# Expert retrieval of an encoder layer: a one-hot part on ScalarE, other shares of gathered rows for DVE and TensorE, V loaded four tiles at a time

## The reference

```python
D_MODEL, SEQ, PEER_HEADS, PEER_KEYS, PEER_TOPK = 1024, 1024, 8, 128, 16

def reference(x, c, ...):
    ...                                   # adaLN modulation, HGRN2 and convolution groups, w_out
    hn2 = _modulate(_rmsnorm(h, norm_ffn_g[l]), sh2, sc2)
    ffn = _peer(hn2, peer_wq[l], peer_keys1[l], peer_keys2[l], peer_u[l], peer_v[l])
    h = h + g2[:, None, :] * ffn
    ...                                   # final RMSNorm, shift and scale

def _peer(h, wq, keys1, keys2, u_tab, v_tab):
    q = (h @ wq).reshape(nb, L, PEER_HEADS, PEER_DKEY)
    s1, s2 = ...                          # scores of both halves of q against 128 keys each
    v1, i1 = lax.top_k(s1, PEER_TOPK); v2, i2 = lax.top_k(s2, PEER_TOPK)
    cand = v1[..., :, None] + v2[..., None, :]
    sc, ci = lax.top_k(cand, PEER_TOPK)   # 16 of 16384 experts for each head
    e = i1[ci // 16] * PEER_KEYS + i2[ci % 16]
    w = jax.nn.softmax(sc, axis=-1)
    # for each token, over its 128 experts:
    act = gelu(sum_d h[t, d] * u_tab[e[t, j], d])
    y[t] = sum_j (w[t, j] * act) * v_tab[e[t, j]]
```

## Time and profile before

| | us |
|---|---|
| median of 3 runs (lowest to highest) | 3291.83 (3290.16 to 3292.69) |
| the profiled execution | 3279.82 |
| its span, first to last instruction | 3278.1 |
| PE busy, DVE busy, ScalarE busy | 2959.7, 2363.2, 553.7 |
| mean granted clock of TensorE | 0.945 |

### The profile page before, as it was taken

One profiled execution on the slowest core, in us unless ns is written; L12 is line 12 of the kernel. 1 busy time (PEld: TensorE's weight loads), 2 busy tenths in 40 slices (PEclk: granted clock), 3 DMA queues, 4 the chain that ended last, 5 costly groups with the idle time before them and its releaser, 6 DMA issues. The chain is left out here.

```text
span 3278.1 us, 31019 instructions
## 1 busy us (share of the span) xinstructions
PE 2959.7 (90%) x10396; PEld 1592.4 (49%) x10396; DVE 2363.2 (72%) x4478; ACT 553.7 (17%) x682; POOL 1220.6 (37%) x1104
## 2 busy tenths in 40 slices
PE   6999699759689997899999999996899998999995
PEld 2557577547475443444554454443344443444442
DVE  4796445530587889999999998886677666776674
ACT  3011443321221100222221221221000000000003
POOL 0111111021124545344333335554455454555550
PEclk8998899869798998999999999998899999999997
DMA  4441111013237999899899899999999999999993
GB/s 184 175 161 35 58 32 34 26 53 108 84 96 296 412 414 337 308 322 348 304 333 333 311 324 379 414 415 408 392 402 399 402 400 402 401 400 402 399 378 141
DMA packets 299657, 919.78 MB, mean 281 GB/s; under 512 B 27376, under 2 KB 76784, under 8 KB 296176
## 3 DMA queue, kind: packets, MB, share of 16 engines
q0 software_dynamic: 147456, 536.94, 42.6%
q1 hardware_dynamic: 113408, 301.76, 25.1%
q10 hardware_dynamic: 38640, 79.18, 6.3%
HBM read 830.21 MB, written 87.56 MB: 280 GB/s over the span
## 5 line engine op out<-in xcount | busy, mean ns | idle before, releaser
L1451 PE MATMUL s_pu<-s_hn,s_ut 128*128 128x512 f32 x2304 | 1017.1, 597 | 7.5 <-ACT s_gst L1562 5.2
L1406 POOL DMA_INDIRECT s_slot<-in_u,s_row x512 | 516.6, 1009 | 714.7 <-DVE s_slot L1807 628.8
L1406 POOL DMA_INDIRECT s_slot<-in_v,s_row x512 | 551.3, 1077 | 452.8 <-DVE s_hB L1820 348.1
L1451 PEld LDWEIGHTS s_pu<-s_hn,s_ut 128*128 128x128 f32 x2304 | 437.4, 192 | 543.7 <-issue 539.8
L1807 DVE SCALAR_TENSOR_TENSOR s_slot<-s_slot,s_ph 128x1024 f32<-128x1024 f32 x512 | 612.5, 1220 | 104.1 <-DMA s_slot<-in_u,s_row 85.0
L1820 DVE SCALAR_TENSOR_TENSOR s_hB<-s_slot,s_dot,s_hB 128x1024 f32<-128x1024 f32 x445 | 561.8, 1284 | 128.0 <-DMA s_slot<-in_v,s_row 127.4
L296 PE MATMUL s_ps<-hn_hi,w_hi 128*128 128x512 f32 x704 | 290.9, 413 | 93.5 <-PEq L270 57.1
L1536 PE MATMUL s_pw<-s_ct,s_vt 128*128 128x512 f32 x512 | 249.1, 610 | 49.5 <-DVE s_ct L1828 25.1
L297 PE MATMUL s_ps<-hn_lo,w_hi 128*128 128x512 f32 x704 | 282.0, 401 | 0.0
L1536 PE MATMUL s_ph<-s_ct,s_vt 128*128 128x512 f32 x512 | 242.5, 596 | 16.0 <-DVE s_slot L1807 16.0
L1536 PE MATMUL s_pu<-s_ct,s_vt 128*128 128x512 f32 x512 | 242.2, 595 | 0.0
(11 more groups left out here) (280 smaller groups left out, 2994.7 us busy)
## 6 DMA issues: line engine op xcount, KB each, us to landing
s_ut<-in_u_tiles SPq DMA_DIRECT2D x128, 512.0 KB, 7.2
s_vt<-in_v SPq DMA_DIRECT2D x128, 512.0 KB, 24.0
s_g<-s_gst ACTq DMA_DIRECT2D x128, 256.0 KB, 7.0
s_w<-s_wb ACTq DMA_DIRECT2D x16, 2048.0 KB, 10.9
s_gr<-s_g SPq DMA_DIRECT2D x64, 512.0 KB, 23.7
s_wr<-s_w SPq DMA_DIRECT2D x16, 2048.0 KB, 46.6
s_ada<-in_ada SPq DMA_DIRECT2D x48, 512.0 KB, 5.4
s_x<-in_xT SPq DMA_DIRECT2D x16, 512.0 KB, 4.0
```

The costliest lines, as they stand in the source:

```text
L1406: pool.indirect_dma_start(out=slot[s][:, :], out_offset=None, in_=io[kind], in_offset=bass.IndirectOffsetOnAxis(ap=row[b][:, j:j + 1], axi ...
L1451: mm = pe.matmul(pu[:, n % 2, :], ut[n % UR][:, k, :], hn[:, k, :], start=(k == 0), stop=(k == DC - 1))
```

## The change

ScalarE makes the third weighted part, `hotw[..][2]`, in 8 activations of 128 columns with the remainder of the weight (`rest`, fp32) as scale; DVE makes two parts in place of three, and `hot1` has two buffers. PE waits for this part with a semaphore of its own (`third_ready`), and the cast of the third part falls away. PE gets 48 side rows, DVE 976 rows in all in place of 960. `sparse_by` gives 164 rows by tile 20, 387 by tile 97, 507 by tile 122 and 537 by tile 127. V comes in 32 loads of four tiles (2 MB, 16 KB runs, from a copy of V laid out for that), into two slots.

```diff
-SIDE_ROWS = 64
+SIDE_ROWS = 48
...
     for t in range(-QT, n + 1):
-        tenths += (45 if t < RANK_AT else 42 if t < HOT_AT[0] else
-                   26 if t < RANK_AT + RANK_TILES * (len(RANKED) - MADE_PICKS) else 47 if t < 123 else 60)
+        tenths += (45 if t < RANK_AT else 44 if t < HOT_AT[0] else
+                   29 if t < RANK_AT + RANK_TILES * (len(RANKED) - MADE_PICKS) else 48 if t < 123 else 60)
...
-    VR = 8
+    VG, VR = 4, 2
...
-    hot1 = at("s6_hot1", [P, 4, KEYS, 2], BF16, F0 + 48 * KB)
+    hot1 = [at(f"s6_hot1{s}", [P, 4, KEYS, 2], BF16, F0 + (48, 60)[s] * KB) for s in range(2)]
...
-    vt = [at(f"s6_vt{s}", [P, D], F32, F0 + 4 * KB * s) for s in range(VR)]
+    vt = [at(f"s6_vt{s}", [P, VG, D], F32, F0 + 4 * VG * KB * s) for s in range(VR)]
...
             def load_v(n):
+
                 if n >= VR:
-                    sp.wait_ge(v_done, n - VR + 1)
-                sp.dma_start(vt[n % VR][:, :], io["v"][n * P:(n + 1) * P, :]).then_inc(v_in[n % VR], 16)
+                    sp.wait_ge(v_done, VG * (n - VR + 1))
+                sp.dma_start(vt[n % VR][:, :, :], io["v_tiles"][n]).then_inc(v_in[n % VR], 16)
...
-            for n in range(KEYS - VR):
-                load_v(n + VR)
+            for n in range(KEYS - VG * VR):
+                if n % VG == VG - 1:
+                    load_v(n // VG + VR)
...
             def place_batch(a, r):
                 n = 16 * a + r
                 pe.wait_ge(hot_ready, n + 1)
+                pe.wait_ge(third_ready, n + 1)
...
-                pe.wait_ge(v_in[n % VR], 16 * (n // VR + 1))
+                pe.wait_ge(v_in[n // VG % VR], 16 * (n // (VG * VR) + 1))
...
+            def third_parts(a, r):
+                n = 16 * a + r
+                act.wait_ge(hot1_ready, n + 1)
+                if n >= 2:
+                    unit = UNITS * ((n - 2) // 16) + 2 + 2 * ((n - 2) % 16)
+                    act.wait_ge(pw_full[unit % 2], unit // 2 + 1)
+                for i in range(8):
+                    q, t = divmod(i, 2)
+                    o = act.activation(hotw[n % 2][2][:, q, :, t], hot1[n % 2][:, q, :, t], ACT.Copy,
+                                       scale=rest[:, 1, 8 * r + i:8 * r + i + 1])
+                o.then_inc(third_ready, 1)
...
+                for a, r in hot_batches(n - 1):
+                    third_parts(a, r)
                 for a, r in hot_batches(n - 2):
                     evacuate(a, r)
...
-                dve.tensor_copy(wT[2][:, :], rest[:, 1, :])
-                dve.drain()
...
-                dve.tensor_tensor(hot1[:, :, :, :], keys, spread(keyT[0]), ALU.is_equal)
+                dve.tensor_tensor(hot1[n % 2][:, :, :, :], keys, spread(keyT[0]), ALU.is_equal).then_inc(hot1_ready, 1)
                 dve.tensor_tensor(hot2[n % 2][:, :, :, :], keys, spread(keyT[1]), ALU.is_equal)
                 dve.drain()
-                for x in range(3):
-                    dve.tensor_tensor(hotw[n % 2][x][:, :, :, :], hot1[:, :, :, :], spread(wT[x]), ALU.mult)
+                for x in range(2):
+                    dve.tensor_tensor(hotw[n % 2][x][:, :, :, :], hot1[n % 2][:, :, :, :], spread(wT[x]), ALU.mult)
...
+        "v_tiles": a["peer_v"][0].reshape(KEYS // 4, 4, KEYS, D).transpose(0, 2, 1, 3),
```

More of the change, by code:

```diff
@@ L1299, in step6 @@
     keyT = [small(f"keyT{s}", [P, P], BF16) for s in range(2)]
-    wT = [small(f"wT{x}", [P, P], BF16) for x in range(3)]
+    wT = [small(f"wT{x}", [P, P], BF16) for x in range(2)]
     rest = small("rest", [P, 2, P])
@@ L1321, in step6 @@
         sd_made, sd_taken, sd_stored = sem("s6_sd_made"), sem("s6_sd_taken"), [sem(f"s6_sd_stored{s}") for s in range(2)]
-        hot_ready = sem("s6_hot_ready")
+        hot_ready, hot1_ready, third_ready = sem("s6_hot_ready"), sem("s6_hot1_ready"), sem("s6_third_ready")
         pw_full = [sem(f"s6_pw_full{s}") for s in range(2)]
@@ L1535, in _ @@
                             pe.wait_ge(taken, number["u", SPARSE - 1, P - 1] + 1)
-                    mm = pe.matmul(bank(c), vt[n % VR][:, c * P:(c + 1) * P], ct[:, n % CR, :],
+                    mm = pe.matmul(bank(c), vt[n // VG % VR][:, n % VG, c * P:(c + 1) * P], ct[:, n % CR, :],
                                    start=(n == 0), stop=(n == KEYS - 1))
```

## The result

The changed kernel takes 3261.08 us (median of 3 runs, 3254.38 to 3263.82); the kernel before took 3291.83 (3290.16 to 3292.69). The ratio is 0.990, with a 95% interval of 0.9884 to 0.9916: 31 us faster. The time lies inside the range (3233 to 3271), but 15 us above the forecast of 3246 and 3 above the likeliest case's own range (3234 to 3258). The profiled execution took 3261.08 with a span of 3259.4, only 18.7 less than the profiled execution of before (3279.8). That difference misleads, as the second trace of before shows further down.

What follows compares the result with a forecast made beforehand. It took PE and DVE as full from 1307 to 1985 us, then DMA, then PE with waits for V. 0 - 16.0 - 22.4 - 7.6 = -46.0 us from 3291.8 gave 3246; range 3233 to 3271 with 8 of 10.

Steps and rivals of the forecast that it cites:

- the likeliest case: The forecast itself for the whole kernel: 3246 us, own range 3234 to 3258, chance 0.66.
- start of products: End of first phase: DVE's products start at 2286 as now, change 0, bounds 2280 and 2295 (-6 to +9).
- Part by part, first phase: DVE, ScalarE and PE up to the last u tile: it ends 8 to 14 us sooner, worth nothing by itself.
- the 12 us of room: At tile 93 PE could place its batch 12 us earlier before it waits for DVE.
- These cancel: DVE by tile 97: 30 us saved on weighted parts against 31 us spent on 26 more u rows.
- The stall (-16.0): PE's 15.97 us idle after the first V tile goes, as no u row stands between products: -16.0 us.
- the waits for V (-22.4, -7.6): V phase: 22.4 of 24.4 us of PE's waits and 7.6 of 8.9 us of slow running go.
- V is on time, and PE becomes the bound: V phase: with V at 320 GB/s, eight tiles' loads take 54.5 us, under PE's 54.9.
- (a): V loads: large rows get only half the bytes, no larger share; about -24 us, 3268; chance 0.14.
- (b): Phase change: ScalarE or the `take_y` wait delays DVE by 9 us, few V waits stay; -32 us, 3260; chance 0.08.
- (c): From 1985 to 3220 us full DMA engines are the bound whatever PE waits for; no gain, 3290; chance 0.05.
- (d): V phase: V's halved headway makes it slower, +65 us or 3357; chance 0.07 together with dear third parts.

Runs made afterwards that it cites:

- the second trace of before: The kernel before, unaltered, run and profiled once more: 3290.0 us, ratio 1.0 (0.9987 to 1.0012); profiled execution 3298.2 us, span 3296.5.

## Why the prediction came out as it did

The direction and the mechanism in the V phase were right. The term that was mis-sized is the start of products, put at 0: against the trace that the sum was made from the u tiles come no earlier, and the chain behind them is 17 us longer. Counted from u tile 0 the start is 14 to 18 us later; -46 with that gives -32 to -28, an estimate from one trace of before, and -31 was measured.

*Part by part, first phase.* "PE then ends the u tiles 8 to 14 us sooner, about 2250" is the step that came out short. PE gained 10 us from tile 24 to tile 97 (652 us to 642 and 643), near the 12 us of room that I gave it. The four rows ahead of the first batch cost the 5 us that I had named: tiles 0 to 24 take 205 us, for 200 in the three other traces with the old quota, though the first trace of before has 206. Behind tile 97, where I had nothing, the change has 279 and 282 us for 270 in the first trace of before; PE waits there 3.5 and 10.9 us for ScalarE, where the first trace of before shows no such wait. From tile 0 to tile 127 that is 1127 and 1131 us, for 1129 in the first trace: no gain. The second trace of before, with 31 us for its stop taken off, has 1136, so 5 to 9 us sooner by that one. "These cancel" holds for DVE's time (30 us saved, 31 spent on rows), but with the new quota DVE is the pace-maker from tile 24 to 97: without ScalarE's part the end is 26 us later. I had priced the whole first phase at 0. A row made there is 0.52 MB that need not be moved later. Against the second trace of before the change has 9 MB less left at 2350 us, 22 us at the line's 2.47; against the first only 2 MB, 5 us, so the size of this gain is open. The ScalarE part cost 2.5 us a batch for the 3.1 taken; the slow end of its bounds is excluded.

*Start of products: 0, bounds -6 to +9.* Measured +31 by the first pair of traces, outside the bounds; by the second pair PE's V matmuls start 2.4 us later (2314.7, 2312.3), in them, but only since that trace of before has the stop at 2250. With the stops out of it, it is +14 to +18, above the bounds. I had named the chain of the last u tile, `take_y`, 25 rows and products, and its 30.5 us; it takes 39 (2275.2 to 2313.9), since most rows come 1.7 us apart and not 1.22. And I relied on PE ending at 2250, where it ended at 2276 and 2273; 17 and 10 us of that are the stop at 1030 us, absent in my trace. What the step cost the end is another matter: with the wait gone the kernel is some 9 us faster by the medians, not 27.

*The stall (-16.0) and the waits for V (-22.4, -7.6).* All three happened: no stall, 0.9 to 4.0 us of waits, 883 to 887 us from first to last matmul for the 886 forecast, V loads by turns of packets. "V is on time, and PE becomes the bound" holds as it stands: PE is busy 881.5 of 883 us. What it left out is how narrow that is. The same phase started at 2288 is 901 us long, and at 2265, with 25 more rows in it, 921: PE and the transfers are both near their limit there. And the gain isn't V's alone: the V edit by itself brings 14 us, the third part and the rows the other 18.

*Base.* The sum was made against 3279.8 and the distance of 12 us kept. That was right, and in part luck: the distance is in all likelihood the stop at 1030 us, which all other traces have and the prediction did not know of. The measured 31 us are 15 less than 46.

*Rivals.* (a) falls: 16-KB rows had 1.36 MB against 0.33, 4-KB rows 0.83 against 0.81. The Trainium skill, "DMA: Bandwidth & Descriptors" (Queues, rings and completion order; SWDGE vs HWDGE), has a packet of typically 9 to 17 descriptors, preferably at most 4096 B, drained before the engine turns to the next queue. The prediction drew from the 4096 B that long rows bring no larger share, and the measurement decides against that. Turns of several descriptors each would also give the nearly equal counts seen, so the runs don't speak against that part. (b) is what happened: its wait for `take_y`, at 33.6 and 36.6 us, and its time, 3260, for 3261; it had 0.08. Its late start is larger than its 9 us, and its waits for V smaller. That the forecast of 3246 still has the result in its wide range is owed to (a) and (b) being taken into it. (c) falls by its time, but it named the full DMA engines, which is what an earlier start of V runs into. (d) falls for 16-KB rows; with 4-KB rows two slots did lose 14 us against eight.

Open: why PE stops at 1030 us and, in two traces of 14, at 2250 us, and why the first profiled execution of before has neither. The gathers fill the DMA engines in the stop at 2250; whether that is its cause or its effect isn't shown, and whether PE waits there for its own instructions wasn't looked at. Nothing was tried on either.

## What to carry to other kernels

Where several engines and the transfers are all near their limit, count for each edit the bytes that it moves out of the last full stretch, not only the waits that it removes: here 2.47 us a MB, fitted afterwards, has the end of each of the ten traces with 16-KB rows within 4 us. It is no forecast until the bytes are known: a quota that was to move 8 MB moved 2.3. Removing a wait ahead of such a stretch brings only what the stretch doesn't take back, here some 9 of 27 us. An engine that was relieved may bring little until its quota is raised: here 0.2%, within the intervals, and 0.7% with the larger quota. And take a second trace before resting bounds of a few us on one: two executions of one kernel differed by 25 us in where a phase began.

## What the runs showed that was not expected

- PE can have no wait that the profile shows and still take 33 us for 24 matmuls of 128x128 (usual 1.54 us), at clock 0.50 (1.2 GHz), while DVE and the DMA engines work on. It happened in the last batch of the first phase in two traces.
- Weights in 1-KB rows and gathers in 4-KB rows share at 1 to 3.5 in bytes (1.81 and 6.38 MB), V in 16-KB rows and gathers at 4 to 1 (1.36 and 0.33), in one kernel.
- ScalarE makes a 128x128 bf16 product with a scale for each row in 0.31 us apiece when eight stand in a row (8 in 2.49 us), and in 0.30 with sixteen (4.82), though one is listed with 424 ns.
